# Two decoder layers in fp32 on one core: four weight pieces left unsplit and held in idle tiles, x normed by a diagonal matmul, and the weight splits of the layer change in another order

## The chip, the cores and the metric

One core of one Trainium2 chip runs the whole program, in one launch. The time is what one execution takes on the device, in microseconds (us); the median over several executions counts. The kernel before takes 334.11 us, the median of 3 runs (333.4 to 334.76).

## What is computed

The reference is a trunk of two layers over 256 tokens of width 1024, all in fp32. Cut to what matters:

```python
c_act = silu(c)
for layer in range(2):
    shift, scale, gate = split(c_act @ w_mod[layer] + b_mod[layer], 3)
    hdn = rms_norm(x, norm_w[layer]) * (1 + scale) + shift
    q1, k1, v1, g1, q2, k2, v2, g2 = split(hdn @ w_in[layer], 8)      # 8 groups of 512 columns
    y1, y2 = mixers of the layer      # layer 0: differential and dilated attention
                                      # layer 1: block-sparse and stick-breaking attention
    y = concatenate([y1 * silu(g1), y2 * silu(g2)]) @ w_out[layer]
    x = x + gate * y
```

`w_in` is 1024 x 4096 and `w_out` 1024 x 1024 per layer. The first gate `g1` multiplies the first 512 of the 1024 mixed columns, the second gate `g2` the last 512.

## The kernel before, in words

**Pieces and steps.** Each layer's weights come as ten chunks of 512 columns, in the order K1, Q1, V1, K2, Q2, V2, G1, G2, O0, O1 (O0 and O1 are the halves of `w_out`). A chunk has four pieces p = 0 to 3 of 256 rows, each a raw tile of 128 x 1024 fp32, 512 KB. A layer is a hand-written list of 80 steps (`steps_of`, L37): a step is one piece for one half s of the result (s is mostly the token half), with two contraction blocks of 128. Steps are counted through: 0 to 79 are layer 0, 80 to 159 layer 1. Pieces are numbered 0 to 79 in the order of their first step: 24 to 27 are G1, 28 to 31 G2, 32, 33, 34 and 38 are O0 (p = 0, 1, 2, 3), 35, 36, 37 and 39 are O1, and 40 to 47 are K1 and Q1 of layer 1. The steps at the end of layer 0 are: 48 to 55 G1, 56 to 59 G2 s=0, 60 to 63 G2 s=1, then 64 to 66 O0 p0, p1, p2 and 67 to 69 O1 p0, p1, p2 and 70, 71 O0 p3, O1 p3 for s=0, then 72, 73 O0 p0, p1, 74, 75 O1 p0, p1, 76, 77 O0 p2, p3, 78, 79 O1 p2, p3 for s=1. The blocks that the second gate has multiplied are the contraction rows of p = 2 and 3.

**Split and unsplit.** A split piece is written as two tiles of type fp32r: `w_hi` is a rounded copy that ScalarE (ACT) makes (`split_hi`, L448), `w_lo` the rest, a subtraction on VectorE (DVE) (`split_lo`, L722). The activations `hy_hi` and `hy_lo` are made in the same way. TensorE (PE) takes three fp32r matmuls for each product (`mm3`, L1051). A piece in `PLAIN` (L68) stays as it came and PE multiplies it in fp32 with the unsplit activations `y`; in the profile one fp32 matmul is two records. Eight buffers hold split pieces. `EARLY` and `CHANGE_HI` (L109, L111) and `hi_at` (L115) say in which step the split is made: ACT's half in `hi_at`, DVE's one step later (`lo_at`), never before the piece whose buffer it takes has had its last step.

**The queues.** SP issues every load. It walks one list (`loads`, L382): the raw pieces, and 48 modulation tiles of `w_mod`, 512 KB each, which DVE multiplies by the conditioning and sums (`take_mod`, L733; 24 of them lie one in each odd step from 25 to 71, `MOD_AT`, L176). Load number i goes into one of seven raw buffers (`RAW`) and waits for the reader of load i-7: `w_lo` for a split piece, the last step for an unsplit one, `take_mod` for a modulation tile. All engines walk the same steps in order and never skip ahead. ACT, within a step, first takes what PE has turned or mixed, then scores, tiles, gates, and last the `w_hi` of the step. DVE does the x update of the step first, then the scores, norms, gates, `w_lo`, and last the modulation tile. Attention runs in pairs of heads between the projection steps (`PAIR_AT`, L164: pairs 4 to 7 start in steps 46, 50, 54, 58).

**Gates.** `gate_lags` (L191) gives the steps in which the sigmoid, the product with y (`gate_product`, L906), `hy_hi` and `hy_lo` (`gate_low`, L920) are made; `project` (L1218) waits on `y_lo_ok` ahead of each step of O0 and O1.

**The layer change.** O0 and O1 are added into x by DVE (`update_x`, L928), ACT squares x, and the reciprocal root of each token ends in `x_t`. DVE then scales x (1024 columns) into `xn`, which lies in the tile `kT` (L1032), PE transposes four blocks into the bank `turned` and four into `mixed` (`turn_x` L1097, `mix_x` L1105, behind steps 75 and 83, `X_AT`), DVE and ACT apply scale and shift and split the result for layer 1. At the start of the kernel ACT scales one half of x and DVE the other (L498, L800), and `first_turn` (L1159) turns it: twice before step 0 and twice inside the stream.

Of the kernel before, what the change touches and what calls it, by code (L numbers as in the profile page):

```python
# [64 lines left out]
ORDER = sorted(PIECE, key=PIECE.get)  # L65


PLAIN = (18, 19, 20, 21, 22, 23, 25, 26)  # L68
SPLIT = [n for n in range(len(FIRST)) if n not in PLAIN]


# [34 lines left out]

EARLY = {24: 14, 27: 16, 28: 14, 29: 13, 30: 12, 31: 11}  # L109

CHANGE_HI = {40: 73, 41: 74, 42: 77, 43: 79, 44: 80, 45: 81, 46: 82, 47: 83}  # L111

# [169 lines left out]
def program(nc, x, w_mod, w, a_lambda, vectors, consts, out):  # L284
    with ExitStack() as ctx:
# [52 lines left out]
        bias = qn[:, :, :].rearrange("p a b -> p (a b)").rearrange("p (i s) -> p i s", i=4)  # L338

        y_tok = gt[:, :, :].rearrange("p a b -> p (a b)").rearrange("p (h t d) -> p h t d", h=4, t=2)  # L340

        xn = kT[:, :, :, :].rearrange("p a b c -> p (a b c)").rearrange("p (t f) -> p t f", t=2)
        junk = [a[:, :, :].rearrange("p a b -> p (a b)") for a in (qn, gt)]

        proj = [bank(f"proj{i}") for i in range(4)]
# [4 lines left out]
        def bank_of(layer, c, side):  # L350
# [11 lines left out]
        mix_ok, mix_act, mix_dve = sem("mix_ok"), sem("mix_act"), sem("mix_dve")  # L362
        mod_done, ab_ok, gate_col = sem("mod_done"), sem("ab_ok"), sem("gate_col")
        c_T, c_ok = sem("c_T"), sem("c_ok")
        x_sq, x_ln, x_seed, x_seed2, x_sum, x_rms, xn_ok = (
            sem(n) for n in ("x_sq", "x_ln", "x_seed", "x_seed2", "x_sum", "x_rms", "xn_ok"))
        h_pre, h_hi_ok, h_ok = sem("h_pre"), sem("h_hi_ok"), sem("h_ok")
        sq_ok, ms_ok, n_ln, n_seed, n_seed2, rn_ok, qn_ok = (
            sem(n) for n in ("sq_ok", "ms_ok", "n_ln", "n_seed", "n_seed2", "rn_ok", "qn_ok"))
# [6 lines left out]
        y_ok, y_hi_ok, y_lo_ok = sem("y_ok"), sem("y_hi_ok"), sem("y_lo_ok")  # L376
        upd, out_ok, stored = sem("upd"), sem("out_ok"), sem("stored")
        dve_step = sem("dve_step")


        mods = [m for group_ in FIRST_MODS for m in group_] + LATER_MODS
        loads = []  # L382
        for p in range(4):
            loads += [("mod", m) for m in FIRST_MODS[p]] + [("w", n) for n in range(3 * p, 3 * p + 3)]
        later = [(FIRST[n] if n in PLAIN else hi_at(n), 1, ("w", n)) for n in range(12, len(FIRST))]
        later += [(at - 1, 0, ("mod", m)) for at, m in zip(MOD_AT, LATER_MODS)]
        loads += [key for _, _, key in sorted(later)]
# [19 lines left out]
        @block.sync  # L407
        def _(sp):
            sp.dma_start(rows[:, :], vectors).then_inc(vec_in, 16)
            sp.dma_start(cst[:, C_ID:C_ID + P], consts[:, C_ID:C_ID + P]).then_inc(id_in, 16)  # L410
            sp.dma_start(xs[:, :, :], x[0].rearrange("(t p) f -> p t f", p=P)).then_inc(x_in, 16)
            for i, key in enumerate(loads):
                if i >= RAW:
                    was = loads[i - RAW]
                    if was[0] == "mod":
                        sp.wait_ge(mod_done, mods.index(was[1]) + 1)
                    else:
                        n = was[1]
                        if n in PLAIN:
                            wait_step(sp, LAST[n])  # L420
                        else:
                            sp.wait_ge(lo_done, split_count(n))
                whence = w_mod[mods.index(key[1])] if key[0] == "mod" else w[key[1]]
                sp.dma_start(raw_tile(key), whence.rearrange("p (k n) -> p k n", k=2)).then_inc(raw_full[i % RAW], 16)
                if key == ("w", 2):
                    sp.dma_start(lam, a_lambda.rearrange("a i d -> a (i d)").broadcast_to([P, 4 * HD])
                                 .rearrange("p (i d) -> p i d", i=4)).then_inc(lam_in, 16)
                if key == ("w", 11):
                    sp.dma_start(cst[:, C_TRI:], consts[:, C_TRI:]).then_inc(cst_in, 16)
            for i, (t, c) in enumerate((t, c) for t in range(2) for c in range(2)):  # L430
                sp.wait_ge(out_ok, i + 1)
                sp.dma_start(out[0, t * P:(t + 1) * P, c * CH:(c + 1) * CH],
                             xs[:, t, c * CH:(c + 1) * CH]).then_inc(stored, 16)
            sp.wait_ge(stored, 64)

        @block.scalar
        def _(act):
# [56 lines left out]
            act.wait_ge(x_sq, 1)  # L494
            act.wait_ge(x_sum, 1)
            rms_seed(x_ms[:, 0:2], x_y[:, 0:2], x_t[:, 0:2], x_ln, x_seed, x_seed2, 1)
            act.wait_ge(x_rms, 1)
            nc.scalar.activation(xn[:, 0, :], xs[:, 0, :], ACT.Copy, scale=x_t[:, 0:1]).then_inc(xn_ok, 1)  # L498
            first_blocks(0)
            act.wait_ge(vec_c, 2)  # L500
            nc.scalar.activation(v[:, V_LAM + 2:V_LAM + 4], v[:, V_LAM:V_LAM + 2], ACT.Exp).then_inc(act_c, 1)
# [103 lines left out]
            for layer in range(LAYERS):  # L605
                for g in range(STEPS):
# [80 lines left out]
                    for c in (G1, G2):  # L687
                        for s in range(2):
                            n = 4 * layer + 2 * (c - G1) + s
                            if done_at(layer, c, s) + gate_lags(c, s)[0] == at:  # L690
                                act.wait_ge(g_sig, n + 1)
                                nc.scalar.activation(gt[:, s, :], gt[:, s, :], ACT.Exp).then_inc(g_gate, 1)
                            if done_at(layer, c, s) + gate_lags(c, s)[2] == at:
                                act.wait_ge(y_ok, n + 1)

                                if c == G2:
                                    wait_step(act, done_at(layer, G2, 1))
                                blk = 2 * (n % 4)
                                to = 8 + blk if c == G1 else blk
                                nc.scalar.activation(hy_hi[:, to:to + 2, :], y[:, blk:blk + 2, :], ACT.Copy).then_inc(y_hi_ok, 1)  # L700
# [9 lines left out]
        def _(dve):  # L710
# [86 lines left out]
            dve.wait_ge(x_seed2, 1)  # L797
            refine(x_ms[:, 0:2], x_y[:, 0:2], x_t[:, 0:2]).then_inc(x_rms, 1)
            dve.wait_ge(x_rms, 1)
            nc.vector.tensor_scalar_mul(xn[:, 1, :], xs[:, 1, :], x_t[:, 1:2]).then_inc(xn_ok, 1)  # L800
            first_blocks(0)
            dve.wait_ge(lam_in, 16)
            for i in range(2):
# [116 lines left out]
            def gate_low(layer, c, s):  # L920

                n, blk, _, _, ys = gate_of(layer, c, s)
                to = 8 + blk if c == G1 else blk
                dve.wait_ge(y_hi_ok, n + 1)
                nc.vector.tensor_tensor(hy_lo[:, to:to + 2, :], ys, hy_hi[:, to:to + 2, :],  # L925
                                        ALU.subtract).then_inc(y_lo_ok, 1)

# [10 lines left out]
            for layer in range(LAYERS):  # L938
                for g in range(STEPS + layer):
# [61 lines left out]
                    for c in (G1, G2):  # L1001
                        for s in range(2):
# [2 lines left out]
                                gate_sigmoid(layer, c, s)  # L1005
                            if done_at(layer, c, s) + product == at:
                                gate_product(layer, c, s)
                            if done_at(layer, c, s) + low == at:
                                gate_low(layer, c, s)
                    if at == 44:  # L1010
                        nc.vector.tensor_scalar_mul(mask_id[:, :], ident, MASKED)
# [11 lines left out]
                    for t in range(2):  # L1023
# [4 lines left out]
                        if at == X_SEED[t]:  # L1028
                            dve.wait_ge(x_seed2, 2 + t)
                            dve.wait_ge(x_sum, 2 + t)  # L1030
                            link(refine(x_ms[:, 2 * t:2 * t + 1], x_y[:, t:t + 1], x_t[:, t:t + 1]))
                            nc.vector.tensor_scalar_mul(xn[:, t, :], xs[:, t, :], x_t[:, t:t + 1]).then_inc(xn_ok, 1)  # L1032

        @block.gpsimd
        def _(pool):
# [11 lines left out]
        def _(pe):  # L1047
# [48 lines left out]

            def turn_x(t):  # L1097

                pe.wait_ge(xn_ok, 3 + t)
                turned_left(("x", t))  # L1100
                for k in range(4):
                    i = nc.tensor.transpose(turned[:, k * P:(k + 1) * P], xn[:, t, k * P:(k + 1) * P], ident)
                i.then_inc(turn_ok, 1)

            def mix_x(t):  # L1105

                mixed_left(("x", t))
                for k in range(4):
                    i = nc.tensor.transpose(mixed[:, k * P:(k + 1) * P], xn[:, t, (4 + k) * P:(5 + k) * P], ident)
                i.then_inc(mix_ok, 1)  # L1110

            def two_heads(grp, blk, slots):
# [46 lines left out]
            def first_turn(p):  # L1159
# [3 lines left out]
                    (turned_left, mixed_left)[p % 2](key)  # L1163
                for a in range(2):
                    for t in range(2):
                        s = nc.tensor.transpose(b[:, a * S + t * P:a * S + (t + 1) * P],
                                                xn[:, t, (2 * p + a) * P:(2 * p + a + 1) * P], ident)
                s.then_inc((turn_ok, mix_ok)[p % 2], 1)

            def scores(j):  # L1170
# [47 lines left out]
            def project(layer, g):  # L1218
# [10 lines left out]
                    pe.wait_ge(h_ok, p + 1)  # L1229
                if layer == 1 and c == K1 and p in (0, 2):  # L1230
                    pe.wait_ge(h_ok, 5 + 2 * s + p // 2)
                if c >= O0:
                    pe.wait_ge(y_lo_ok, 4 * layer + p + 1)
                if at == FIRST[n]:
                    if plain:
                        wait_raw(pe, ("w", n))
# [38 lines left out]
                    s = nc.tensor.transpose(proj[half][:, i * P:(i + 1) * P], v[:, m:m + 1].broadcast_to([P, P]), ident)  # L1275
                s.then_inc(c_T, 1)
            pe.wait_ge(cols_ok, 1)
            pe.wait_ge(xn_ok, 2)
            first_turn(0)
            first_turn(1)  # L1280
            pe.wait_ge(c_ok, 2)
# [100 lines left out]
```

## Time and profile before

| | |
|---|---|
| median of 3 runs | 334.11 us |
| profiled execution | 334.44 us, its span 332.6 us |
| PE busy (matmul) | 296.6 us, 89% |
| DVE busy | 240.2 us, 72% |
| ACT busy | 202.8 us, 61% |
| DMA | 70.30 MB, mean 211 GB/s |
| chain that ended last | PE 52%, DVE 25%, ACT 12%, DMA 6% |

The span is the time from the first to the last instruction of one profiled execution. A row of the timeline is an instruction or a run of equal ones, with the idle time ahead of it in brackets and what ended it. The chain of waits goes back from the last instruction, at each step to what released it. PEclk is the clock that TensorE was granted in a stretch, as a share of 2.4 GHz. PE's matmuls are pipelined, so a record overlaps the next.

### The profile page before, as it was taken

The numbers are of one execution on the slowest core, as the hardware profiler recorded it, in microseconds if no ns is written. First come the engines' busy times: TensorE is split into PE (matmuls) and PEld (weight loads), VectorE is DVE, ScalarE is ACT, GpSimd is POOL, SyncE is SP. The second block draws the span as 40 slices with busy tenths as digits, with TensorE's granted clock in tenths as the row PEclk, the third lists the DMA queues.
The fourth block names the chain that finished last, engine by engine and source line by source line (L and its number), as shares of the span: only waits on it lengthen the run. The fifth ranks groups of instructions, "written<-read, shape, count | busy, mean of one in ns | idle before, by whom it ended". The sixth has DMA issues, their size and how long they took to land.

```text
span 332.6 us, 4776 instructions
## 1 busy us (share of the span) xinstructions
PE 296.6 (89%) x1693; PEld 238.2 (72%) x1693; DVE 240.2 (72%) x487; ACT 202.8 (61%) x406; POOL 12.2 (4%) x20
## 2 busy tenths in 40 slices
PE   2299998999989989797989699999999999988895
PEld 2177776776555768685777478888887799887683
DVE  3899999879783763799878756979773544469533
ACT  4634588555565757998157635576664796897300
POOL 0000000000005440000000000000000000000000
PEclk9999999999999999989999979999999999999999
DMA  7999999563687496386854717578647246100011
GB/s 258 366 415 410 408 405 360 183 235 104 239 310 257 164 367 230 96 291 231 287 167 143 241 67 224 171 299 283 198 163 263 73 145 207 48 17 2 0 63 63
DMA packets 19878, 70.30 MB, mean 211 GB/s; under 512 B 2192, under 2 KB 2576, under 8 KB 19856
## 3 DMA queue, kind: packets, MB, share of 16 engines
q1 hardware_dynamic: 19856, 70.01, 58.6%
q8 instruction: 13, 0.21, 0.2%
q14 instruction: 9, 0.07, 0.1%
HBM read 68.95 MB, written 1.05 MB: 210 GB/s over the span
## 4 chain that ended last, share of the span: by engine, by line
PE 52%; DVE 25%; ACT 12%; DMA 6%; issue 4%; SPq 0%; DVEq 0%; ACTq 0%
PE proj L1049 36%; PE score L1049 8%; DVE w_lo L725 7%; DVE raw L741 6%; DMA raw<-in_w 5%; PE mixed L1049 3%; ACT w_hi L453 2%; PE turned L1094 2%; PE turned L1076 2%; DVE y L918 1%; DVE gt L910 1%; DVE xs L935 1%; DVE hy_lo L925 1%; DVE sq L932 1%; DVE probs L993 1%
## 5 line engine op out<-in xcount | busy, mean ns | idle before, releaser
L725 DVE TENSOR_TENSOR w_lo<-raw,w_hi 128x1024 fp32r<-128x1024 f32 x72 | 87.1, 1220 | 14.9 <-ACT w_hi L453 14.6
L453 ACT ACTIVATE w_hi<-raw 128x1024 fp32r<-128x1024 f32 x72 | 74.9, 1050 | 17.0 <-DMA raw<-in_w 15.4
L1049 PE MATMUL proj<-w_hi,hy_hi 128*128 128x512 f32 x152 | 63.4, 417 | 10.1 <-DVE hy_lo L775 6.0
L1049 PE MATMUL proj<-w_lo,hy_hi 128*128 128x512 f32 x152 | 60.7, 400 | 0.0
L1049 PE MATMUL proj<-w_hi,hy_lo 128*128 128x512 f32 x152 | 60.7, 399 | 0.0
L741 DVE CUSTOM_DVE_ANT_0 raw<-raw,c_rows 128x1024 f32<-128x1024 f32 x48 | 57.8, 1223 | 0.0
L1049 PE MATMUL proj<-hy_hi,w_hi 128*128 128x256 f32 x176 | 53.1, 302 | 0.0
L1049 PE MATMUL proj<-hy_lo,w_hi 128*128 128x256 f32 x176 | 50.4, 287 | 0.0
L1049 PE MATMUL proj<-hy_hi,w_lo 128*128 128x256 f32 x176 | 50.4, 286 | 0.0
L1049 PEld LDWEIGHTS proj<-w_hi,hy_hi 128*128 128x128 f32 x152 | 29.4, 194 | 19.1 <-issue 5.1
L1049 PEld LDWEIGHTS proj<-hy_hi,w_hi 128*128 128x128 f32 x176 | 34.3, 195 | 2.1 <-issue 2.1
L1049 PEld LDWEIGHTS proj<-hy_lo,w_hi 128*128 128x128 f32 x176 | 34.3, 195 | 0.2 <-issue 0.2
L1049 PEld LDWEIGHTS proj<-hy_hi,w_lo 128*128 128x128 f32 x176 | 34.3, 195 | 0.0
L1049 PEld LDWEIGHTS proj<-w_hi,hy_lo 128*128 128x128 f32 x152 | 29.4, 193 | 6.7
L1049 PEld LDWEIGHTS proj<-w_lo,hy_hi 128*128 128x128 f32 x152 | 29.4, 193 | 5.5
L555 ACT ACTIVATE probs<-logits,stat 128x128 f32<-128x128 f32 (+1 forms) x48 | 21.3, 447 | 9.4 <-DVE stat L825 9.4
L1049 PE MATMUL proj<-raw,y 128*128 128x512 f32 x48 | 22.4, 595 | 0.0
L522 ACT ACTIVATE probsT<-turned 128x384 f32<-128x384 f32 x20 | 9.7, 483 | 18.3 <-PE turned L1094 18.2
L1049 PE MATMUL score<-w_hi,hy_hi 128*128 128x512 f32 x48 | 18.8, 391 | 0.0
L1049 PE MATMUL score<-w_lo,hy_hi 128*128 128x512 f32 x48 | 18.7, 389 | 0.0
L1049 PE MATMUL score<-w_hi,hy_lo 128*128 128x512 f32 x48 | 18.7, 389 | 0.0
L862 DVE TENSOR_REDUCE n_ms<-sq 128x8 f32<-128x512 f32 (+1 forms) x13 | 9.4, 726 | 12.7 <-ACT sq L589 11.2
(142 smaller groups left out, 402.6 us busy)
## 6 DMA issues: line engine op xcount, KB each, us to landing
raw<-in_w SPq DMA_DIRECT2D x80, 512.0 KB, 4.6
raw<-in_w_mod SPq DMA_DIRECT2D x48, 512.0 KB, 5.6
xs<-in_x SPq DMA_DIRECT2D x1, 1024.0 KB, 5.1
out_x<-xs SPq DMA_DIRECT2D x4, 256.0 KB, 2.0
cst<-in_constants SPq DMA_DIRECT2D x1, 520.0 KB, 6.4
logits<-in_a_lambda SPq DMA_DIRECT2D x1, 128.0 KB, 11.7
rows<-in_vectors SPq DMA_DIRECT2D x1, 64.0 KB, 1.9
cst<-in_constants SPq DMA_DIRECT2D x1, 64.0 KB, 2.1
```

The costliest lines, as they stand in the source:

```text
L453: nc.scalar.activation(w_hi[:, slot(n), :, :], raw_tile(("w", n)), ACT.Copy).then_inc(hi_done, 1)
L522: nc.scalar.activation(probsT[:, (2 * j + o) % 4, :], turned[:, 0:MAPW], ACT.Copy).then_inc(turn_act, 1)
L555: i = nc.scalar.activation(probs[:, M % 4, cs], logits[:, M % 2, cs], ACT.Exp, scale=-1.0, bias=st[:, tile:tile + 1], accum_out=st[:, 2 + ...
L725: nc.vector.tensor_tensor(w_lo[:, slot(n), :, :], raw_tile(("w", n)), w_hi[:, slot(n), :, :], ALU.subtract).then_inc(lo_done, 1)
L741: nc.vector.tensor_tensor_reduce(out=tile, in0=tile, in1=c_rows[:, :], scale=1.0, scalar=0.0, op0=ALU.mult, op1=ALU.add, accum_out=col(V_M ...
L862: nc.vector.reduce_sum(n_ms[:, n % 2, heads * s:heads * s + heads], src.rearrange("p (h d) -> p h d", h=heads), axis=AX.X).then_inc(ms_ok, 1)
L910: nc.vector.tensor_tensor(g, b[:, :], g, ALU.mult).then_inc(free_dve, 1)
L918: nc.vector.tensor_tensor(ys, ys, g.rearrange("p (a s) -> p a s", a=2), ALU.mult).then_inc(y_ok, 1)
L925: nc.vector.tensor_tensor(hy_lo[:, to:to + 2, :], ys, hy_hi[:, to:to + 2, :], ALU.subtract).then_inc(y_lo_ok, 1)
L1049: return nc.tensor.matmul(o, a, b, start=start, stop=stop, skip_group_check=True)
L1076: i = nc.tensor.transpose(turned[:, b * P:(b + 1) * P], qn[:, s, b * P:(b + 1) * P], ident)
L1094: i = nc.tensor.transpose(turned[:, b * P:(b + 1) * P], probs[:, (2 * j + o) % 4, b * P:(b + 1) * P], ident)
```

## The change

Four pieces of layer 0, 34, 37, 38 and 39 (O0 and O1 of p = 2 and 3, the rows of the second gate), are no longer split. They are loaded into the halves of the tiles `qT` and `kT`, by four loads that SP issues in a row once step 59 is done, ahead of the modulation tile of step 61. `hy_hi` and `hy_lo` of the second gate of layer 0 are not made any more; the steps wait for y itself. Splits have other steps: `w_hi` of 32, 33, 35, 36 in 49, 51, 53, 58 (before: 56, 57, 59, 61), of 40 to 47 in 67, 68, 69, 70, 74, 76, 79, 80 (before: 73, 74, 77, 79 to 83). Since the list of loads is sorted by those steps, loads change places too. x is no longer scaled: DVE multiplies the identity by `x_t` (`x_diagonal`), and a fp32 matmul with that diagonal takes the place of each transpose. ACT has no part in it at the start.

```diff
+HELD = (34, 37, 38, 39)
+HELD_FROM = 59
+PLAIN = (18, 19, 20, 21, 22, 23, 25, 26, 34, 37, 38, 39)
-EARLY = {24: 14, 27: 16, 28: 14, 29: 13, 30: 12, 31: 11}
-CHANGE_HI = {40: 73, 41: 74, 42: 77, 43: 79, 44: 80, 45: 81, 46: 82, 47: 83}
+EARLY = {24: 14, 27: 16, 28: 14, 29: 13, 30: 12, 31: 11, 32: 15, 33: 14, 35: 14, 36: 10}
+CHANGE_HI = {40: 67, 41: 68, 42: 69, 43: 70, 44: 74, 45: 76, 46: 79, 47: 80}
...
+def in_parts(layer, c):
+    return layer == 1 or c == G1
...
+        x_diag = sb("x_diag", [P, 2, P])
-        xn = kT[:, :, :, :].rearrange("p a b c -> p (a b c)").rearrange("p (t f) -> p t f", t=2)
...
-        later = [(FIRST[n] if n in PLAIN else hi_at(n), 1, ("w", n)) for n in range(12, len(FIRST))]
+        later = [(FIRST[n] if n in PLAIN else hi_at(n), 1, ("w", n)) for n in range(12, len(FIRST)) if n not in HELD]
...
+        behind_held = next(key for at, _, key in later if at > HELD_FROM)
+        held = [a[:, i, :, :].rearrange("p a b -> p (a b)").rearrange("p (k n) -> p k n", k=2) for a in (qT, kT) for i in range(2)]
...
             for i, key in enumerate(loads):
+                if key == behind_held:
+                    wait_step(sp, HELD_FROM)
+                    for n, b in zip(HELD, held):
+                        sp.dma_start(b, w[n].rearrange("p (k n) -> p k n", k=2)).then_inc(held_in[HELD.index(n)], 16)
...
-            act.wait_ge(x_rms, 1)
-            nc.scalar.activation(xn[:, 0, :], xs[:, 0, :], ACT.Copy, scale=x_t[:, 0:1]).then_inc(xn_ok, 1)
             first_blocks(0)
...
-                            if done_at(layer, c, s) + gate_lags(c, s)[2] == at:
+                            if in_parts(layer, c) and done_at(layer, c, s) + gate_lags(c, s)[2] == at:
...
+            def x_diagonal(t):
+                nc.vector.tensor_scalar_mul(x_diag[:, t, :], ident, x_t[:, t:t + 1]).then_inc(diag_ok, 1)
...
-            nc.vector.tensor_scalar_mul(xn[:, 1, :], xs[:, 1, :], x_t[:, 1:2]).then_inc(xn_ok, 1)
+            for t in range(2):
+                x_diagonal(t)
...
-                            if done_at(layer, c, s) + low == at:
+                            if in_parts(layer, c) and done_at(layer, c, s) + low == at:
...
-                            nc.vector.tensor_scalar_mul(xn[:, t, :], xs[:, t, :], x_t[:, t:t + 1]).then_inc(xn_ok, 1)
+                            x_diagonal(t)
...
-                    i = nc.tensor.transpose(turned[:, k * P:(k + 1) * P], xn[:, t, k * P:(k + 1) * P], ident)
+                    i = mm(turned[:, k * P:(k + 1) * P], xs[:, t, k * P:(k + 1) * P], x_diag[:, t, :], True, True)
...
-                if c >= O0:
-                    pe.wait_ge(y_lo_ok, 4 * layer + p + 1)
+                if c >= O0 and plain:
+                    pe.wait_ge(y_ok, 4 * layer + p + 1)
+                elif c >= O0:
+                    pe.wait_ge(y_lo_ok, 2 * layer + p + 1)
```

`mix_x` and `first_turn` change as `turn_x` does.

## Rows read from the trace of the kernel before

**Rows 1.** Windows, steps 58 on: us, busy per engine (count), clock, DMA share, GB/s.

```profile
136.20:151.30 15.10, 11.26 (x79) 10.46 (x80) 14.79 (x30) 14.47 (x32) 0.00 (x0) 0.89 0.69 240
...
151.30:171.10 19.80, 17.95 (x83) 13.78 (x81) 17.17 (x32) 9.05 (x19) 0.00 (x0) 1.00 0.73 242
...
171.10:195.98 24.88, 21.75 (x94) 17.30 (x95) 19.20 (x30) 14.82 (x28) 0.00 (x0) 0.93 0.51 170
```

**Rows 2.** Timeline of PE: start us, us, what, [idle before <-releaser]; first, step 50.

```profile
112.95 1.89 PE L1049 MATMUL proj<-y,raw 128*128 128x256 f32 x8
...
119.35 1.99 PE L1049 MATMUL proj<-y,raw 128*128 128x256 f32 x8 [1.11 <-DMA raw<-in_w]
...
136.19 0.55 PE L1094 MATMUL turned<-cst,probs 128*128 128x128 f32 x3 [0.57 <-ACT probs L564]
...
140.03 0.52 PE L1094 MATMUL turned<-cst,probs 128*128 128x128 f32 x3 [1.87 <-ACT probsT L522]
...
151.06 0.52 PE L1094 MATMUL turned<-cst,probs 128*128 128x128 f32 x3 [1.97 <-ACT probsT L522]
...
155.98 0.50 PE L1049 MATMUL proj<-w_hi,hy_hi 128*128 128x512 f32 x1 [0.84 <-DVE hy_lo L925]
...
171.13 0.66 PE L1102 MATMUL turned<-cst,kT 128*128 128x128 f32 x4 [1.04 <-DVE kT L1032]
...
184.48 0.66 PE L1102 MATMUL turned<-cst,kT 128*128 128x128 f32 x4 [1.24 <-DVE kT L1032]
...
191.54 0.64 PE L1049 MATMUL proj<-w_hi,hy_hi 128*128 128x512 f32 x1 [1.86 <-DVE w_lo L725]
```

**Rows 3.** Windows behind three gaps of PE, columns as in rows 1.

```profile
17.10:21.05 3.95, 3.95 (x9) 3.11 (x10) 3.76 (x7) 1.27 (x3) 0.00 (x0) 1.00 1.02 418
...
140.00:144.00 4.00, 3.97 (x21) 4.00 (x22) 3.90 (x9) 3.97 (x12) 0.00 (x0) 0.57 0.90 305
...
191.50:195.30 3.80, 3.76 (x10) 2.94 (x11) 1.51 (x3) 0.60 (x1) 0.00 (x0) 0.55 0.41 138
```

**Rows 4.** Chain of waits: two split steps, an unsplit one, gate rows, transposes.

```profile
62.13 2.77 PE proj L1049 x12
...
94.16 1.72 PE proj L1049 x4
...
95.88 0.89 PE mixed L1049 x8
...
98.49 0.45 PE turned L1076 x4
```

**Rows 5.** Timeline of SP's queue, issues of two modulation loads.

```profile
114.53 0.33 SPq L424 DMA_DIRECT2D raw<-in_w_mod  x1
...
118.47 0.33 SPq L424 DMA_DIRECT2D raw<-in_w_mod  x1
```

**Rows 6.** DMA view around the issues of rows 5; last, us to landing.

```profile
raw<-in_w_mod SPq DMA_DIRECT2D x1, 512.0 KB, 3.1
...
raw<-in_w_mod SPq DMA_DIRECT2D x1, 512.0 KB, 5.6
```

**Rows 7.** Timeline of DVE, the modulation rows of steps 47 and 49.

```profile
113.28 1.21 DVE L741 CUSTOM_DVE_ANT_0 raw<-raw,c_rows 128x1024 f32<-128x1024 f32 x1
...
117.21 1.22 DVE L741 CUSTOM_DVE_ANT_0 raw<-raw,c_rows 128x1024 f32<-128x1024 f32 x1
```

**Rows 8.** Chain of waits on DVE: one w_lo, one hy_lo, the scaling of x.

```profile
154.18 1.14 DVE w_lo L725
...
155.32 0.60 DVE hy_lo L925
...
170.32 0.75 DVE kT L1032
```

**Rows 9.** Groups by line and shape: busy us, mean ns of one.

```profile
L852 DVE TENSOR_SCALAR probs<-probs,stat 128x128 f32<-128x128 f32 x8 | 2.3, 286 | 0.3
```

**Rows 10.** Page, the 40 slices: what the DMA engines moved.

```profile
GB/s 258 366 415 410 408 405 360 183 235 104 239 310 257 164 367 230 96 291 231 287 167 143 241 67 224 171 299 283 198 163 263 73 145 207 48 17 2 0 63 63
```

More of the change, by code:

```diff
@@ L65 @@
 ORDER = sorted(PIECE, key=PIECE.get)
-PLAIN = (18, 19, 20, 21, 22, 23, 25, 26)
+HELD = (34, 37, 38, 39)
+HELD_FROM = 59
+PLAIN = (18, 19, 20, 21, 22, 23, 25, 26, 34, 37, 38, 39)
 SPLIT = [n for n in range(len(FIRST)) if n not in PLAIN]
@@ L364, in program @@
         c_T, c_ok = sem("c_T"), sem("c_ok")
-        x_sq, x_ln, x_seed, x_seed2, x_sum, x_rms, xn_ok = (
-            sem(n) for n in ("x_sq", "x_ln", "x_seed", "x_seed2", "x_sum", "x_rms", "xn_ok"))
+        x_sq, x_ln, x_seed, x_seed2, x_sum, x_rms, diag_ok = (
+            sem(n) for n in ("x_sq", "x_ln", "x_seed", "x_seed2", "x_sum", "x_rms", "diag_ok"))
         h_pre, h_hi_ok, h_ok = sem("h_pre"), sem("h_hi_ok"), sem("h_ok")
@@ L378, in program @@
         dve_step = sem("dve_step")
+        held_in = [sem(f"held_in{i}") for i in range(len(HELD))]
         mods = [m for group_ in FIRST_MODS for m in group_] + LATER_MODS
@@ L384, in program @@
             loads += [("mod", m) for m in FIRST_MODS[p]] + [("w", n) for n in range(3 * p, 3 * p + 3)]
-        later = [(FIRST[n] if n in PLAIN else hi_at(n), 1, ("w", n)) for n in range(12, len(FIRST))]
+        later = [(FIRST[n] if n in PLAIN else hi_at(n), 1, ("w", n)) for n in range(12, len(FIRST)) if n not in HELD]
         later += [(at - 1, 0, ("mod", m)) for at, m in zip(MOD_AT, LATER_MODS)]
-        loads += [key for _, _, key in sorted(later)]
+        later.sort()
+        loads += [key for _, _, key in later]
+        behind_held = next(key for at, _, key in later if at > HELD_FROM)
         place = {key: i for i, key in enumerate(loads)}
+        held = [a[:, i, :, :].rearrange("p a b -> p (a b)").rearrange("p (k n) -> p k n", k=2) for a in (qT, kT) for i in range(2)]
         def raw_tile(key):
+            if key[0] == "w" and key[1] in HELD:
+                return held[HELD.index(key[1])]
             return raw[:, place[key] % RAW, :, :]
         def wait_raw(eng, key):
+            if key[0] == "w" and key[1] in HELD:
+                return eng.wait_ge(held_in[HELD.index(key[1])], 16)
             eng.wait_ge(raw_full[place[key] % RAW], 16 * (place[key] // RAW + 1))
@@ L923, in gate_low @@
                 to = 8 + blk if c == G1 else blk
-                dve.wait_ge(y_hi_ok, n + 1)
+                dve.wait_ge(y_hi_ok, n + 1 - 2 * layer)
                 nc.vector.tensor_tensor(hy_lo[:, to:to + 2, :], ys, hy_hi[:, to:to + 2, :],
@@ L1097, in turn_x @@
             def turn_x(t):
-                pe.wait_ge(xn_ok, 3 + t)
+                pe.wait_ge(diag_ok, 3 + t)
                 turned_left(("x", t))
                 for k in range(4):
-                    i = nc.tensor.transpose(turned[:, k * P:(k + 1) * P], xn[:, t, k * P:(k + 1) * P], ident)
+                    i = mm(turned[:, k * P:(k + 1) * P], xs[:, t, k * P:(k + 1) * P], x_diag[:, t, :], True, True)
                 i.then_inc(turn_ok, 1)
@@ L1108, in mix_x @@
                 for k in range(4):
-                    i = nc.tensor.transpose(mixed[:, k * P:(k + 1) * P], xn[:, t, (4 + k) * P:(5 + k) * P], ident)
+                    i = mm(mixed[:, k * P:(k + 1) * P], xs[:, t, (4 + k) * P:(5 + k) * P], x_diag[:, t, :], True, True)
                 i.then_inc(mix_ok, 1)
@@ L1165, in first_turn @@
                     for t in range(2):
-                        s = nc.tensor.transpose(b[:, a * S + t * P:a * S + (t + 1) * P],
-                                                xn[:, t, (2 * p + a) * P:(2 * p + a + 1) * P], ident)
+                        s = mm(b[:, a * S + t * P:a * S + (t + 1) * P],
+                               xs[:, t, (2 * p + a) * P:(2 * p + a + 1) * P], x_diag[:, t, :], True, True)
                 s.then_inc((turn_ok, mix_ok)[p % 2], 1)
@@ L1277, in _ @@
             pe.wait_ge(cols_ok, 1)
-            pe.wait_ge(xn_ok, 2)
+            pe.wait_ge(diag_ok, 2)
             first_turn(0)
```

## The prediction

> **What bounds the kernel now.** I read the windows first. In [rows 1] the stretch around the last third of layer 0 shows TensorE (PE) idle: 11.26 us busy of 15.10, 17.95 of 19.80, 21.75 of 24.88, while VectorE (DVE) is busy 14.79 and 17.17 in the first two; ScalarE (ACT) too is nearly full in the first (14.47). So there DVE, and before it ACT, set the pace. Next PE's own timeline [rows 2]: of its rows two see no gap or a DMA, the others wait for ACT (0.57, 1.87, 1.97) or DVE (0.84, 1.04, 1.24, 1.86). The last is the final wait of the layer change; behind it PE runs nearly without gaps for some 60 us, so what PE has gained or lost at 195 us reaches the end.
>
> With the 1.11 at 119.35 the eight gaps sum to 10.5. A record is drawn longer than its work (three transposes 0.52 [rows 2], where four take 0.45 [rows 4]), so a true gap is some 0.15 longer: 11.7. Two gaps cost twice: behind 1.87 and 1.86 the granted clock is 0.57 and 0.55 [rows 3], that is mostly the lower of TensorE's two levels (1.2 instead of 2.4 GHz). 4.00 x 0.43 and 3.80 x 0.45 make 1.7 each. **Between step 50 (112.95) and 195.3, PE now loses 11.7 + 3.4 = 15.1 us.** The change is judged against that.
>
> **What the edits remove.** Four w_lo on DVE at 1.14 [rows 8] and their w_hi on ACT; two hy_lo at 0.60 and their hy_hi. Four more w_lo (32, 33, 35, 36) leave the full stretch for steps 50 to 59. DVE has the w_lo of 32 to 39 between 135 and 158; all but that of 36 leave this stretch, so it is relieved by 7 x 1.14 + 2 x 0.60 = 9.2 us, and no longer sets the pace there. The ACT gaps in [rows 2] shrink: before 140.03 ACT sheds two w_hi of about 1 us, so 2.0 becomes about 0.5; before 151.06 it sheds all, 2.1 becomes 0.2. No w_hi stands ahead of 136.19 any more: gap 0.
>
> **What they add on PE.** A split step is 2.77 / 2 = 1.385, an unsplit one 1.72 [rows 4]: 0.335 x 8 steps (66, 69, 70, 71, 76 to 79) = 2.7. Turning x at steps 75 and 83: eight transposes are 2 x 0.45 = 0.9; eight fp32 matmuls of that shape go by the gate rows, 8 records for 4 matmuls in 0.89 [rows 4], 1.8. So 0.9 more, twice: 1.8. **Added work 4.5.** TensorE: Matmul & The Clock Gate, Terms, in the Trainium skill, calls the transpose mode four times faster for fp32, where the trace shows two times; by that page each turn would cost 2.6 more, not 0.9.
>
> On DVE the scaling of 1024 columns (0.75, [rows 8]) becomes a diagonal of 128, 0.29 by the nearest shape [rows 9]: 0.45 less, twice, on the path to the turn. At the start ACT's scaling goes and DVE makes both diagonals, 0.3 sooner at best; the next weight split waits for its load and the DMA then runs near its top, 415 GB/s [rows 10], so I take 0.1. Bounds 0 and 0.7. The two first turns inside the stream cost PE 0.45 each, where it waits afterwards for hy_lo.
>
> **What is moved, and the queue it is moved past.** All raw loads share SP's queue and seven buffers; load i waits for the reader of load i-7. Pieces 32 and 33 now come ahead of 25 and 26. Counting the list: piece 25 had waited for w_lo of piece 29 and stood ready at 112.95; now its buffer is that of the modulation load which DVE takes in step 47. That instruction starts at 113.28 [rows 7], and the load issued right behind it goes at 114.53 [rows 5]. Landing of a first load after a quiet queue is 3.1 us [rows 6], so 117.6: **PE waits 4.7 us at step 50**, unhidden, since PE is in order and the scores of pair 5 stand behind it. Bounds 3.1 and 4.4. Behind the 4.02 gap at 17.10 nine records fill 3.95 us [rows 3], where 17 would fit at the speed of [rows 4]: half speed, 1.9 us lost. I take that here. Piece 26 now waits for the modulation load of step 49 (117.21, [rows 7]) and so takes the place of the load issued at 118.47 [rows 5], which lands 5.6 later [rows 6], 124.1. PE comes at 119.35 - 1.1 + 4.7 + 1.9 = 124.8, later: the old gap of 1.25 is gone. PE is 5.35 late.
>
> Then the three ACT gaps give back 0.7, 1.5 and 1.9, and the slow clock behind 140.03 another 1.7, 5.8 in all. Step 64 began behind the transposes of 151.06, at 151.3; PE now reaches it at 151.3 + 5.35 - 5.8 = 150.9.
>
> **The held pieces.** SP waits for the end of step 59 (140.03 less its gap of 2.0, plus 5.35 - 0.7: 142.7) and issues four held loads before the modulation load of step 61; DVE needs that before it can write hy_lo for step 64. Five loads of 0.52 MB: at 415 GB/s 1.26 each, 3.1 + 4 x 1.26 = 8.1 us at best. At worst: the fourth of the earlier burst landed at 118.47 + 5.6, 9.5 after the first was issued, and a fifth makes 10.8. I take 9.0, nearer the burst than full rate: 151.7. DVE adds 1.14 and 0.60: step 64 starts at 153.5, a gap of 2.6. Step 65 waits for y and the second hy_lo (1.35 + 0.6): a gap of 0.6. Behind them DVE has slack; the w_lo of 40 to 43, now before x is updated, fill it.
> At step 75 the last x update of the first half needs step 71, a w_lo, a modulation row and the take of the columns before it. I estimate a gap of 0.7 in place of 1.2, between 0 and 1.5. At step 83 and 87 nothing is late any more: PE has by then become the slower one.
>
> **The sum.** PE loses after: 4.7 + 1.9 + 0.5 + 0.2 + 2.6 + 0.6 + 0.7 = 11.2, plus 4.5 of work = 15.7, against 15.1. That is +0.5 (walking from gap to gap, PE is 1.6 late at step 66, 3.4 at 76, 4.2 at 84, and 0.5 at 88), less 0.1 from the start: **+0.4**. The profiled execution lasted 334.44 (span 332.6) and would become 334.8; the median of the three is 334.11, so 334.5. A measurement of this kernel can tell some 0.5%, 1.7 us, from no change.
>
> **Rivals.** *A second slow clock.* The gap at step 64 is 2.6 us. Gaps of 1.87 and 1.86 were followed by the low level [rows 2, 3], the 1.97 at 151.06 by a clock of 1.00 [rows 1]. If it is, half of what follows is lost again, 1.7 us: 336.2. It decides whether the gap there, with the 0.6 behind it, counts as idle; the evidence is split. 0.25.
> *The burst is slow* (ends the other side too): mod load at 10.8, not 9.0, step 64 late by 1.8: 336.3. From about 10.3 on it is slower by more than the measurement's bound. For it: the one burst whose landings I have. Against: its fourth load was issued 4 us after its first. 0.1.
> *The modulation load is not late, faster.* If it lands within 6.4 us of step 59, DVE is ready before PE: the 2.6 and most of the 0.6 go, 331.4 (6.4 is 150.9 less 1.74 of DVE work less 142.7). Against it stand 415 GB/s as the top rate and the five loads; for it, that they differ in target and that only one of the five is waited for. The page DMA: Bandwidth & Descriptors, Queues, rings and completion order, of the Trainium skill says completion is not first in, first out on an issuing engine; no row here shows a load overtaking another. A shorter wait at step 50 would shift later waits along and give little. I give this, and any other gain of that size, 0.22.
> *Turning costs more.* If an fp32 matmul took four times a transpose's 0.11 [rows 4], the eight would take 3.5, 1.7 more on each turn than in my sum: +3.4, 337.9. The gate rows, whose matmuls have the same shape and type, speak against it. 0.03. It is the rule of TensorE: Matmul & The Clock Gate, Terms, in the Trainium skill.
> *The change does not do what it says*, because the stretch only swaps DVE's wait for DMA's, is in effect my forecast: 0.40.
>
> **Numbers.** 334.5. Range 331.6 to 337.0: it takes in the fast rival, both slow ones alone, and not their coincidence. Faster by over 0.5%: 0.22. Within: 0.45, the forecast and edges of its neighbours. Slower: 0.33.
>
> **What the profile will show.** PE waiting 4 to 5 us for a DMA at step 50, then records of double length; no ACT gap over 1 us between steps 58 and 63; DVE waiting about 4 us for a DMA near 148 to 152, and PE behind it; unsplit steps of 1.72; no PE wait between steps 80 and 88. I am wrong if step 50 starts on time, if DVE takes the modulation load of step 61 without waiting, or if PE stands 2 us or more away from 196 us at step 88.

## The result, and the profile after

| | before | after |
|---|---|---|
| median | 333.75 us (4 runs, 333.29 to 334.76) | 337.90 us (4 runs, 337.51 to 338.29) |
| profiled execution, its span | 334.44, 332.6 | 338.16, 336.4 |
| PE, DVE, ACT busy | 296.6, 240.2, 202.8 us | 303.1, 234.1, 196.3 us |

The kernel became slower: the ratio is 1.0106, 95% interval 1.0078 to 1.0134. I had forecast 334.5 and a range that ended at 337.0, so the prediction was wrong, and by 3.4 us, nearly all of it in one stretch.

PE's timeline after, the rows that answer to [rows 2] (L1120 are the transposes of L1094 before, L951 is L925):

```profile
118.50 3.47 PE L1075 MATMUL proj<-y,raw 128*128 128x256 f32 x8 [4.78 <-DMA raw<-in_w]
...
125.36 1.89 PE L1075 MATMUL proj<-y,raw 128*128 128x256 f32 x8
...
144.04 0.52 PE L1120 MATMUL turned<-cst,probs 128*128 128x128 f32 x3 [0.61 <-ACT probsT L543]
...
151.56 0.52 PE L1120 MATMUL turned<-cst,probs 128*128 128x128 f32 x3
...
155.03 0.50 PE L1075 MATMUL proj<-w_hi,hy_hi 128*128 128x512 f32 x1 [2.96 <-DVE hy_lo L951]
...
157.03 0.80 PE L1075 MATMUL proj<-w_hi,hy_hi 128*128 128x512 f32 x1 [0.17 <-DVE hy_lo L951]
...
160.69 1.98 PE L1075 MATMUL proj<-qT,y 128*128 128x512 f32 x4
...
176.92 1.16 PE L1075 MATMUL turned<-x_diag,xs 128*128 128x128 f32 x8 [0.85 <-DVE x_diag L756]
...
191.15 1.05 PE L1075 MATMUL turned<-x_diag,xs 128*128 128x128 f32 x8
...
199.74 0.39 PE L1075 MATMUL proj<-w_hi,hy_hi 128*128 128x512 f32 x1
```

All eight old gaps are smaller or gone, and two large ones are new: 4.78 for a DMA, 2.96 for DVE. The lateness against the same steps of before can be read off: +6.0 at step 52 (125.36 against 119.35), +4.0 at 144.04, +0.5 at 151.56, +3.7 at step 64 (151.34 before), +4.7 at step 66 (155.98 before), +3.8 at 199.74 (195.98 before). The span grew by those 3.8.

What DVE waited for ahead of step 64 stands in its timeline and in the chain of waits; SP's queue gives the issues:

```profile
153.14 1.22 DVE L766 CUSTOM_DVE_ANT_0 raw<-raw,c_rows 128x1024 f32<-128x1024 f32 x1 [4.48 <-DMA raw<-in_w_mod]
```

```profile
143.46 0.80 SPq L435 DMA_DIRECT2D qT<-in_w  x2
144.65 0.80 SPq L435 DMA_DIRECT2D kT<-in_w  x2
145.50 2.12 SPq L447 DMA_DIRECT2D raw<-in_w_mod  x4
```

```profile
145.50 7.62 DMA raw<-in_w_mod
153.14 1.22 DVE raw L766
154.38 0.60 DVE hy_lo L951
...
157.03 2.92 PE proj L1075 x6
...
178.08 0.89 PE mixed L1075 x8
178.97 3.44 PE proj L1075 x8
```

Step 59 ended at 143.44, the four held loads went first, and the modulation load behind them was there 9.7 us after that end. The last two rows are the prices: eight records, the four fp32 matmuls of half a turn, 0.89; two unsplit steps 3.44.

The windows answer to [rows 1] and [rows 3], columns as there, the last one taken behind the gap of 2.96:

```profile
140.20:155.00 14.80, 11.27 (x92) 9.82 (x91) 10.11 (x25) 13.39 (x34) 0.00 (x0) 1.00 0.71 259
155.00:176.90 21.90, 20.87 (x72) 13.07 (x72) 17.89 (x31) 7.81 (x14) 0.00 (x0) 0.92 0.91 323
176.90:199.70 22.80, 22.78 (x102) 16.85 (x103) 14.39 (x26) 11.26 (x25) 0.00 (x0) 1.00 0.30 99
...
155.00:158.80 3.80, 3.60 (x10) 2.52 (x11) 3.70 (x7) 0.04 (x1) 0.00 (x0) 0.68 1.03 414
```

The edits did relieve DVE: 10.11 busy of 14.80, where it was 14.79 of 15.10. PE gained nothing from it in this stretch: 11.26 busy before, 11.27 after. Its idle time had changed its owner, from ACT and DVE to, for the most part, one late load. The last row is a second slow clock, 0.68.

### The profile page after: what moved, and what is told of

Same layout as the page of the kernel before. It is cut to its first block, busy times and chain, and to the rows that moved or that the text cites. A ratio compares the mean times of both kernels' runs of the same rounds, so it can differ in the third digit from the quotient of the medians.

```text
span 336.4 us, 4790 instructions
## 1 busy us (share of the span) xinstructions
PE 303.1 (90%) x1709; PEld 239.4 (71%) x1709; DVE 234.1 (70%) x482; ACT 196.3 (58%) x399; POOL 13.2 (4%) x20
## 4 chain that ended last, share of the span: by engine, by line
PE 66%; DVE 12%; ACT 9%; DMA 8%; issue 3%; SPq 1%; ACTq 0%; DVEq 0%
PE proj L1075 45%; PE score L1075 12%; DMA raw<-in_w 6%; PE mixed L1075 4%; DVE w_lo L746 3%; DVE raw L766 2%; DMA raw<-in_w_mod 2%; PE turned L1120 2%; PE turned L1102 2%; ACT w_hi L476 2%; DVE probs L1019 1%; ACT logits L687 1%; ACT logits L685 1%; ACT logits L683 1%; DVE xs L961 1%
## 5 line engine op out<-in xcount | busy, mean ns | idle before, releaser
L746 DVE TENSOR_TENSOR w_lo<-raw,w_hi 128x1024 fp32r<-128x1024 f32 x68 | 82.4, 1221 | 16.6 <-ACT w_hi L476 16.2
L476 ACT ACTIVATE w_hi<-raw 128x1024 fp32r<-128x1024 f32 x68 | 70.8, 1051 | 20.6 <-DMA raw<-in_w 19.5
L1075 PE MATMUL proj<-w_hi,hy_hi 128*128 128x512 f32 x144 | 60.5, 420 | 9.7 <-DVE hy_lo L800 5.1
L1075 PE MATMUL proj<-w_hi,hy_lo 128*128 128x512 f32 x144 | 57.4, 398 | 0.0
L1075 PE MATMUL proj<-w_lo,hy_hi 128*128 128x512 f32 x144 | 57.1, 397 | 0.0
L1075 PEld LDWEIGHTS proj<-w_hi,hy_hi 128*128 128x128 f32 x144 | 27.7, 192 | 18.1 <-DVE hy_lo L951 5.8
L1075 PEld LDWEIGHTS proj<-w_hi,hy_lo 128*128 128x128 f32 x144 | 27.6, 192 | 6.2
L1075 PE MATMUL score<-w_hi,hy_hi 128*128 128x512 f32 x40 | 16.1, 402 | 0.0
L1075 PE MATMUL score<-w_hi,hy_lo 128*128 128x512 f32 x40 | 15.6, 390 | 0.0
L1075 PE MATMUL score<-w_lo,hy_hi 128*128 128x512 f32 x40 | 15.6, 389 | 0.0
```

The costliest lines, as they stand in the source:

```text
L476: nc.scalar.activation(w_hi[:, slot(n), :, :], raw_tile(("w", n)), ACT.Copy).then_inc(hi_done, 1)
L746: nc.vector.tensor_tensor(w_lo[:, slot(n), :, :], raw_tile(("w", n)), w_hi[:, slot(n), :, :], ALU.subtract).then_inc(lo_done, 1)
L1075: return nc.tensor.matmul(o, a, b, start=start, stop=stop, skip_group_check=True)
```

## The experiments

Each was timed beside runs of the kernel before on its own chip; the ratios are to those, and the medians of before in the four groups of runs were 333.75, 334.1, 334.1 and 334.6.

**Experiments 1 to 3: the two waits.** Experiment 1 changes only when three of the four early splits are made, and by that the order of the loads:

```diff
-EARLY = {24: 14, 27: 16, 28: 14, 29: 13, 30: 12, 31: 11, 32: 15, 33: 14, 35: 14, 36: 10}
+EARLY = {24: 14, 27: 16, 28: 14, 29: 13, 30: 12, 31: 11, 32: 11, 33: 11, 35: 12, 36: 10}
```

> The changed kernel, with the splits of pieces 32, 33, 35 moved to steps 53, 54, 55, so that their loads stand behind those of pieces 25 and 26 again. Theory of the queue: the wait at step 50 (4.8 us) and the slow records behind it (1.7) go, the old wait of 1.1 before step 52 comes back; PE is 5.3 us earlier at step 60, and the held burst, which hangs on step 59, moves with it: 337.9 - 5.3 = 332.6. Rival (the added TensorE work of unsplit steps and fp32 turns is what costs, waits only swap places): within 1 us of 337.9.

Experiment 2 issues the four held loads further back in SP's queue; their wait for step 59 stays:

```diff
+HELD_BEHIND = 64
-        behind_held = next(key for at, _, key in later if at > HELD_FROM)
+        behind_held = next(key for at, _, key in later if at > HELD_BEHIND)
```

> The changed kernel, with the four held loads issued behind the modulation loads of steps 61, 63, 65 instead of ahead of them; they still wait for step 59. Theory of the queue: VectorE's wait for the load of step 61 (4.5 us) goes, with it TensorE's gap of 3.0 before step 64 and the slow records behind it (1.4): 4.3 us faster, 333.6. Rival (TensorE's added work): within 1 us of 337.9, since the gap would come back before the next step that waits for y.

Experiment 3 has both edits:

> Both edits of e1 and e2. Theory of the queue: the two savings are of different waits and add up, 328.3 to 329.5, well below the kernel before (333.8). Rival: they uncover the same next wait and do not add, 332 or more.

Measured: 332.80 (10 runs; ratio 0.9967, 0.9945 to 0.9989), 334.08 (10 runs; 0.9982, 0.9965 to 0.9999) and 329.23 (4 runs; 0.9847, 0.9822 to 0.9872). PE's timeline of experiment 1:

```profile
119.86 1.99 PE L1075 MATMUL proj<-y,raw 128*128 128x256 f32 x8 [1.00 <-DMA raw<-in_w]
136.71 0.55 PE L1120 MATMUL turned<-cst,probs 128*128 128x128 f32 x3 [0.55 <-ACT probs L585]
139.60 0.52 PE L1120 MATMUL turned<-cst,probs 128*128 128x128 f32 x3 [0.92 <-ACT probsT L543]
150.39 0.54 PE L1075 MATMUL proj<-w_hi,hy_hi 128*128 128x512 f32 x1 [2.75 <-DVE hy_lo L951]
```

The 4.78 at step 50 is gone and the old 1.00 is back, while the gap at step 64 stays. In experiment 2 it is the other way round:

```profile
119.18 3.78 PE L1076 MATMUL proj<-y,raw 128*128 128x256 f32 x8 [4.88 <-DMA raw<-in_w]
145.19 0.52 PE L1121 MATMUL turned<-cst,probs 128*128 128x128 f32 x3 [0.61 <-ACT probsT L544]
```

No other gap follows until x is turned. So the two waits are separate costs: 337.9 - 332.8 = 5.1 us for the load order, 337.9 - 334.1 = 3.8 for the place of the held loads, 8.7 for both together (4.6, 4.1 and 8.7 by the ratios). Without these two waits the change is a gain: experiment 3 is 1.5% faster than the kernel before.

The place of the held loads is two things in one. SP issues in order, so its wait for step 59 holds back every load behind it too, and not only the four transfers stand in the way. In experiment 2 the modulation loads of steps 61, 63 and 65 were issued before that wait; SP's timeline there has no issue between these two rows:

```profile
132.48 0.33 SPq L448 DMA_DIRECT2D raw<-in_w_mod  x1
144.61 0.80 SPq L436 DMA_DIRECT2D qT<-in_w  x2
```

**Experiment 4: the turning of x, with the waits left in.** x is scaled again and transposed. Since kT now receives weights, the scaled x lies in the tile of the values, which is idle then.

```diff
-                nc.vector.tensor_scalar_mul(x_diag[:, t, :], ident, x_t[:, t:t + 1]).then_inc(diag_ok, 1)
+                nc.vector.tensor_scalar_mul(xn[:, t, :], xs[:, t, :], x_t[:, t:t + 1]).then_inc(xn_ok, 1)
-                    i = mm(turned[:, k * P:(k + 1) * P], xs[:, t, k * P:(k + 1) * P], x_diag[:, t, :], True, True)
+                    i = nc.tensor.transpose(turned[:, k * P:(k + 1) * P], xn[:, t, k * P:(k + 1) * P], ident)
```

> The changed kernel with x scaled again and turned by transposes as before (the scaled x in the idle value tile): the fp32 turns undone, all else kept. By my prices TensorE saves 0.9 us on each of two turns and the path to the first turn grows by 0.45: 1.3 us faster, 336.6. If the 0.6 us that the changed kernel loses before step 18 also comes from the turns, 336.0. Rival (a turn costs four times a transpose): 3.4 faster, 334.5.

Measured 337.11 (4 runs, 336.07 to 338.13; ratio 1.0080, 1.0049 to 1.0111). The runs spread by 2 us, so a gain near the expected one is likely but not shown by this run alone. The wait ahead of the first turn is 1.32 where it was 0.85, as the longer scaling makes it; the other gaps are near those of after (4.88, 0.61 and 3.08 for 4.78, 0.61 and 2.96, and none for the 0.17).

**Experiment 5: the diagonal alone, on the kernel before.** The same edit as in the change (the lines of experiment 4 the other way round, in the three places), nothing else.

> The kernel before with one edit: x is turned by fp32 matmuls against a diagonal; pieces, splits and load order stay. Theory (a turn costs 0.9 us more on TensorE and saves 0.45 on VectorE; here VectorE still sets the wait at 191.54, where TensorE idles 1.86 us, and takes the difference up): within 0.4 us of the kernel before, taken as 334.1 + 0.2 = 334.3; the gap of 1.86 shrinks by 0.5 to 1.3. Rival (both turns lie fully on the path of the layer change): +1.8 - 0.9 = +0.9, 335.0. Second question: the first score row of about step 46 came 0.6 us later after the change than before (108.02 against 107.40). If the diagonal at the start does it, it comes at 108.0 here too; if it is the spread of load landings from one execution to the next, either time can appear. Rival of the turning that costs fourfold: 337.5.

Measured 333.13 (10 runs; ratio 0.9971, 0.9954 to 0.9989): slightly faster, below both values expected. PE's timeline:

```profile
151.37 0.52 PE L1098 MATMUL turned<-cst,probs 128*128 128x128 f32 x3 [2.02 <-ACT probsT L521]
...
184.23 1.16 PE L1053 MATMUL turned<-x_diag,xs 128*128 128x128 f32 x8 [0.29 <-DVE x_diag L734]
...
191.32 0.50 PE L1053 MATMUL proj<-w_hi,hy_hi 128*128 128x512 f32 x1 [0.93 <-DVE w_lo L724]
```

and two windows, behind its gaps of 0.93 and of 2.02:

```profile
191.30:195.10 3.80, 3.78 (x17) 3.14 (x18) 1.85 (x3) 1.27 (x2) 0.00 (x0) 1.00 0.43 138
...
151.40:155.20 3.80, 3.80 (x12) 3.09 (x13) 3.80 (x6) 3.74 (x7) 0.00 (x0) 0.58 0.49 156
```

The gap of 1.86 became 0.93, as the theory had it. But behind it the clock in this trace stays at 1.00, where it was 0.55 [rows 3]. PE starts there at 191.32, 0.2 earlier than before, and the span ends 1.8 earlier, so in this pair of traces 1.6 of the 1.8 is the clock. The 0.2 comes from DVE, whose part of the second turn is shorter:

```profile
183.89 0.28 DVE L734 TENSOR_SCALAR x_diag<-cst,x_t 128x128 f32<-128x128 f32 x1
184.09 2.35 DVE L724 TENSOR_TENSOR w_lo<-raw,w_hi 128x1024 fp32r<-128x1024 f32 x2
```

Before, the scaling stood at 183.67 and the w_lo behind it at 184.34: DVE was 0.2 late ahead of this row and is 0.25 early behind it, 0.5 gained.

That the 1.0 us between the medians is the clock's is not shown, and the executions don't bear it out. The mean granted clock of the ten is 0.990, that of the 13 of the kernel before beside them 0.992. Two of the ten ran at 0.998 or more and took 332.4 and 332.8; five of the 13 did, and took 333.2 to 334.1. So on these few a gain of about 1 us is there without any low clock too. The filled gap saved the slow clock in one trace; how much of the 1.0 is due to that, and how much to DVE's shorter step, stays open.

**Experiment 6: the transposes, on experiment 3.** Both load edits, and the lines of experiment 4.

> The version with both load edits (329.2) and x scaled and transposed as before, in a tile that is idle then. TensorE now sets the pace of the layer change, with one gap of 0.85 at the first turn. Theory (each turn in fp32 costs 0.9 on TensorE, scaling instead of a diagonal 0.45 on VectorE, seen only at the first turn): 329.2 - 1.8 + 0.5 = 327.9, range 327.5 to 328.5. Rival (VectorE is as much the bound there, and takes the gain back in later waits): 329.2, no difference. The measured pair of this kind with the waits left in gave 337.9 to 337.1, 0.8 less.

Measured 327.50 (4 runs, 326.98 to 328.04; ratio 0.9794, 0.9773 to 0.9816), the fastest version: 1.7 below experiment 3, near the theory's 327.9 and not the rival's 329.2. Its rows of the page and of the timeline:

```profile
PEclk9999999999999999999999999999999999999999
```

```profile
168.38 0.66 PE L1131 MATMUL turned<-cst,val 128*128 128x128 f32 x4 [1.32 <-DVE val L760]
...
181.87 0.66 PE L1131 MATMUL turned<-cst,val 128*128 128x128 f32 x4
```

No slice of the clock is below 9. One edit thus has both signs: the diagonal gains about 1 us where PE has a gap behind it (experiment 5), and loses 1.7 (1.2 by the spans, 327.4 and 326.2) where PE sets the pace (experiments 3 and 6).

**Experiments 7 and 8: how many loads stand ahead.** Of the four held loads three or two stay ahead of the modulation load of step 61, the others go where experiment 2 put all four (`behind_rest`, by the same HELD_BEHIND = 64). Experiment 7 has AHEAD = 3, experiment 8 has AHEAD = 2:

```diff
-                    for n, b in zip(HELD, held):
+                    for n, b in list(zip(HELD, held))[:AHEAD]:
...
+                if key == behind_rest:
+                    for n, b in list(zip(HELD, held))[AHEAD:]:
+                        sp.dma_start(b, w[n].rearrange("p (k n) -> p k n", k=2)).then_inc(held_in[HELD.index(n)], 16)
```

> The kernel after, with three held pieces ahead of the modulation load of step 61 and the fourth behind it, where e2 put all four. Theory (each held load ahead delays the modulation load by some 1.3 us, 0.52 MB at 415 GB/s, and the wait at step 64 by as much): it is taken 9.7 - 1.3 = 8.4 us after step 59, the gap at step 64 is 2.96 - 1.3 = 1.7, and the 0.17 behind it goes. If a gap of that size still leaves the low level of the clock behind it, 337.9 - 1.3 - 0.2 = 336.4; if the low level goes with it, another 1.5 less, 334.9. Rival (the modulation load's own latency and not the loads ahead makes it late): gap 2.9, 337.9.

> The kernel after, with two held pieces ahead of the modulation load of step 61 and two behind it. Theory: taken 7.1 us after step 59, gap at step 64 2.96 - 2.6 = 0.4, granted clock of 1.00 behind it: 337.9 - 2.6 - 0.2 - 1.5 = 333.6, as with all four behind it (334.1). Rival (the late load costs only its gap, and the low clock comes from elsewhere, a share of DMA near 1.0 in that stretch): 333.6 + 1.5 = 335.1, with a granted clock of 0.6 to 0.7 behind step 64.

Measured 336.12 (10 runs; ratio 1.0051, 1.0018 to 1.0084) and 335.18 (10 runs; 1.0021, 1.0000 to 1.0043). DVE takes the load as follows, first in experiment 7:

```profile
153.19 1.23 DVE L772 CUSTOM_DVE_ANT_0 raw<-raw,c_rows 128x1024 f32<-128x1024 f32 x1 [3.54 <-DMA raw<-in_w_mod]
```

then in experiment 8:

```profile
150.92 1.23 DVE L772 CUSTOM_DVE_ANT_0 raw<-raw,c_rows 128x1024 f32<-128x1024 f32 x1 [1.82 <-DMA raw<-in_w_mod]
```

SP's timeline has the first held load of each, experiment 7 first:

```profile
144.46 0.80 SPq L438 DMA_DIRECT2D qT<-in_w  x2
```

```profile
143.91 0.80 SPq L438 DMA_DIRECT2D qT<-in_w  x2
```

So the first held load was issued at 143.46 with four ahead, 144.46 with three, 143.91 with two. The modulation rows came 9.7, 8.7 and 7.0 us behind it: 1.0 and 1.7 for a load, on the mean the 1.3 of the theory. The rival, a latency that doesn't depend on the loads ahead, is out. PE's timeline at step 64 and behind it, with three ahead:

```profile
155.09 0.50 PE L1081 MATMUL proj<-w_hi,hy_hi 128*128 128x512 f32 x1 [2.01 <-DVE hy_lo L957]
157.08 0.50 PE L1081 MATMUL proj<-w_hi,hy_hi 128*128 128x512 f32 x1 [0.34 <-DVE hy_lo L957]
...
159.49 1.99 PE L1081 MATMUL proj<-qT,y 128*128 128x512 f32 x4
```

and with two:

```profile
152.81 0.50 PE L1081 MATMUL proj<-w_hi,hy_hi 128*128 128x512 f32 x1 [0.29 <-DVE hy_lo L957]
```

The windows: 155.1 to 158.9 with three ahead, 152 to 156 with two.

```profile
155.10:158.90 3.80, 3.46 (x14) 2.28 (x16) 3.69 (x7) 0.41 (x2) 0.00 (x0) 1.00 1.03 418
```

```profile
152.00:156.00 4.00, 3.37 (x15) 2.36 (x15) 3.90 (x9) 2.25 (x4) 0.00 (x0) 1.00 1.02 418
```

Behind 2.01 the clock is 1.00, behind 2.96 it was 0.68, with the same DMA share of 1.0 in all three windows. So a DMA share of 1.0 alone doesn't bring the low level; the idle time ahead is what changed. These are single traces, but all five with a gap here agree: behind the 2.75 of experiment 1 and the 3.08 of experiment 4 the clock is low too, as two windows show, experiment 1 first.

```profile
150.40:154.20 3.80, 3.80 (x10) 2.98 (x11) 3.69 (x7) 0.08 (x1) 0.00 (x0) 0.55 1.02 414
```

```profile
156.20:160.00 3.80, 3.71 (x10) 2.54 (x11) 3.69 (x7) 0.07 (x1) 0.00 (x0) 0.66 1.03 416
```

From step 65 to step 66 the low clock costs (160.69 - 157.03) - (159.49 - 157.08) = 1.25 us. In time, experiment 7 lies between its two values (336.4, 334.9), nearer the one for the low clock, although its trace shows the full clock, for which 334.9 was expected. In that trace the missing 1.2 lies in sizes: PE is 1.0 later than after at the ACT gap (145.04 against 144.04), the gap was to be 1.7 and not 2.01, and none was to follow where 0.34 did. Experiment 8 was to give 333.6 and gave 335.2. That is the number of its rival (335.1), but not its mechanism, which had the clock at 0.6 to 0.7 behind step 64, where it is 1.00: by the trace PE turns x at 173.66, 3.3 us earlier than after, and its span is 3.3 shorter, but its median is only 2.7 lower. The trace of experiment 8 began 0.6 later at step 46, of which below, and left 0.34 at step 65 and 1.08 at the turn, where I had counted 0 and 0.85. Four behind (334.1) is better than two.

## Why the prediction was wrong

**Right.** The wait at step 50: 4.8 for 4.7, at half speed behind it (3.47 for eight records that take 1.89, and 0.15 in the scores: 1.7 for 1.9). Of the +6.0 at step 52, 0.6 was there before step 50, so 5.4 for 5.35. The ACT gap at 144.04, 0.6 for 0.5, and none at 151.56. Both old slow clocks are absent from the trace after. The prices on PE: 1.72 for an unsplit step, 0.89 for four fp32 matmuls, no wait at steps 83 and 87, 0.85 for 0.7 at the first turn. The mechanism of the new wait at step 64, held loads ahead of a modulation load, was the one named, and experiments 2, 7 and 8 bear it out.

**Wrong, in order of size.** With the start I had PE 0.4 late at the row of 195.98, which the prediction calls step 88 (by the count of records it is the first of step 89); it was 3.8 late. The missing 3.4 are these:

- *The clock behind the gap at step 64*, 1.25 us by experiment 7. The step of the sum that failed is "4.7 + 1.9 + 0.5 + 0.2 + 2.6 + 0.6 + 0.7": the 1.9 behind the 4.7 is the slow clock, and behind the 2.6 there is none. It was priced as a rival, "A second slow clock", at 1.7 us and a chance of 0.25. The forecast gap of 2.6 was longer than both of 1.9 behind which the low clock was on record. The one row against, the 1.97 with 1.00 behind, was too little to leave it out.
- *The landing*, 9.7 for 9.0, inside the bounds of 8.1 to 10.8: 0.7.
- *The start*, +0.6 in place of -0.1: 0.7. The first step began 0.3 earlier (16.77 against 17.10), and PE's next waits, all for hy_lo, took it back and more (PE goes on at 47.86 behind one of them, before at 47.22). The score rows of about step 46 start at 107.40 before and at 107.83 in experiment 5, at 108.02 after, and at 108.03 to 108.69 in the other seven. The diagonal isn't the cause, since experiments 4 and 6 have none there and stand at 108.63 and 108.62. Experiments 1, 2, 3, 7 and 8 have the same code as after up to this step, so 0.7 is spread between executions; whether the change adds to it is open.
- *The rest*, 0.7, lies in small pieces: 0.2 ahead of step 64, 0.35 between steps 64 and 66 and 0.2 behind. No run singles them out.

None of them alone leaves the range, and the clock and the landing together would not either: 334.5 + 1.25 + 0.7 = 336.5. It took the start and the small pieces besides, which no rival had priced. All have one sign, and the range took "both slow ones alone, and not their coincidence". The landing and the slow clock aren't independent, since a later load makes a longer gap: behind 2.01 the clock was full, behind 2.75 and more it was low. Whether the forecast 2.6 would have been enough no run shows.

*Readings to correct.* The 1.9 of slow clock at step 50 was priced from the nine records at 17.10, yet [rows 3] prints a clock of 1.00 beside them. Experiment 7's window over seven records of that length, near the same place, reads 0.51:

```profile
17.80:20.99 3.19, 3.19 (x9) 2.54 (x8) 3.15 (x9) 0.37 (x2) 0.00 (x0) 0.51 1.03 419
```

So the length was the better witness there, and the price came out (1.7). That also means the printed mean clock of a trace can leave out this first stretch. And 15.7 against 15.1 is +0.6, not +0.5. Further, the 15.1 counts two slow clocks of the kernel before as fixed. They belong to the trace that was read: 13 of the 51 executions of the kernel before that were timed beside the experiments have a mean granted clock of 0.998 or more, which leaves no room for either.

**Rivals.** The fourfold turn named 337.9, by chance the median measured; its mechanism did not occur. TensorE: Matmul & The Clock Gate, Terms, in the Trainium skill calls the transpose mode four times faster for fp32. The trace shows twice (0.89 against 0.45), and experiments 3 and 6 differ by 1.7 where the page's rule would give 2 x 2.6, less 0.5 for the scaling. "The modulation load is not late" did not occur either, but experiment 2 made it happen: 334.1, where the rival had 331.4. Of the 2.7 between them its trace shows 1.2 as lateness at step 46 (108.60 against 107.40); the other 1.5 is not accounted for.

## What to carry to other kernels

A queue that issues in order turns the place of a load into a time. Four loads that nobody needs yet, and the wait for the step that they hang on, ahead of a load that is due, cost 3.8 us; behind it they left no gap on PE. Judge an edit that lengthens PE's work by the gap behind it: where a gap followed, the longer turns cost nothing (experiment 5); with no gap they cost their full length (experiment 6). When the costs of a range come from one chain (a late load, a longer gap, a slower clock), add them up, don't take them one at a time.

## What the runs showed of the hardware

- The granted clock behind a gap of PE is not told by the gap's length alone near 2 us: 1.86 and 1.87 were followed by 0.55 and 0.57 [rows 3], 1.97 by 1.00, 2.01 by 1.00 (experiment 7), and 2.02 by 0.58 (experiment 5). Behind 2.75, 2.96 and 3.08 (experiment 1, after, experiment 4) it was 0.55, 0.68 and 0.66, behind 0.93 (experiment 5) 1.00.
- It also differs between executions of one kernel. Over the 51 of the kernel before beside the experiments the mean granted clock goes from 0.983 to 1.000; the 13 at 0.998 or more took 333.5 us on the mean, the 17 at 0.986 or less 335.2. One trace can't say what a gap near 2 us costs.

- With four, three and two loads of 0.52 MB ahead in SP's queue, the next one's data was in use 9.7, 8.7 and 7.0 us after the first was issued.
